# A hybrid attention block on eight cores: split exponentials without own waits, norm rows sent through memory, and a new order of chunks and squares

## The reference, cut to what matters

```python
xn = rmsnorm(x, norm_mix_g[l])
u = xn @ w_in[l]                      # b_g, c_g, v_a | q, k, v | gates
y_a = short_gated_conv(b_g, c_g, v_a, conv_w[l]) @ w_a_out[l]
o = diff_attention(q, k, v, lam, slopes)      # 4 heads, two softmax maps each, ALiBi, causal
o = rmsnorm(o, subln_g[l]) * (1.0 - lam_init)
y_b = o.reshape(Bsz, S, DIFF_WIDTH) @ w_b_out[l]
x = x + (g_a * y_a + g_b * y_b) @ w_o[l]
h = rmsnorm(x, norm_mlp_g[l]) @ w_mlp_in[l]
x = x + jnp.square(jax.nn.relu(h)) @ w_mlp_out[l]
return rmsnorm(x, norm_final_g)
```

## Time and profile before

| what | us |
|---|---|
| median of 3 runs (lowest, highest) | 1164.12 (1163.68, 1166.56) |
| the profiled execution's own time | 1163.79 |
| its span on core 5, the slowest (spans of the eight cores 1160.2 to 1162.2) | 1162.2 |
| PE busy in the span | 1127.2 |
| DVE, ACT, POOL busy | 466.9, 550.3, 84.3 |

### The profile page before, as it was taken

The page is one execution under the profiler, slowest core; times in us unless marked ns, Lnnn a source line. Parts: engine busy times, 40 slices in busy tenths (PEclk is TensorE's granted clock), DMA queues, the critical chain, the costliest instruction groups (busy, mean ns, idle before and its releaser), DMA issues.

```text
span 1162.2 us, 20430 instructions; the slowest of 8 cores (1160.2 to 1162.2 us)
## 1 busy us (share of the span) xinstructions
PE 1127.2 (97%) x7162; PEld 563.0 (48%) x7162; DVE 466.9 (40%) x1051; ACT 550.3 (47%) x760; POOL 84.3 (7%) x136
## 2 busy tenths in 40 slices
PE   7999999999999999999999999999999999999997
PEld 3444555455455555555544444444444444444444
DVE  2476666644654632433435544222221322223212
ACT  2585786676666888878523223321231033003301
POOL 5212001001001001001100001000000000000000
PEclk8999999999999999999999999999999999999999
DMA  9877522332067059375296686911210140012001
GB/s 140 166 144 138 144 90 51 110 56 46 5 132 147 19 99 179 65 191 105 38 253 168 207 165 172 158 43 55 70 57 1 55 111 17 19 55 73 2 37 55
DMA packets 67491, 111.46 MB, mean 96 GB/s; under 512 B 37216, under 2 KB 40288, under 8 KB 66368
## 3 DMA queue, kind: packets, MB, share of 16 engines
q0 software_dynamic: 15056, 40.22, 22.5%
q1 hardware_dynamic: 52192, 69.68, 20.0%
q10 hardware_dynamic: 144, 0.26, 0.1%
HBM read 114.40 MB, written 29.36 MB: 124 GB/s over the span
## 4 chain that ended last, share of the span: by engine, by line
PE 92%; ACT 3%; DVE 2%; issue 2%; DMA 1%; POOL 0%; DVEq 0%; ACTq 0%; POOLq 0%
PE ps_all L441 92%; ACT big L715 2%; DMA big<-wv 1%; DVE big L780 0%; DVE big L594 0%; DVE big L604 0%; POOL big L484 0%; ACT big L852 0%; DVE big L772 0%; DVE big L863 0%; DVE big L574 0%; ACT big L592 0%; POOL big L446 0%; DVEq L152 0%; DVE big L571 0%
## 5 line engine op out<-in xcount | busy, mean ns | idle before, releaser
L441 PE MATMUL ps_all<-big 128*128 128x512 bf16 (+7 forms) x7162 | 1127.2, 323 | 28.9 <-ACT big L715 8.2
L441 PEld LDWEIGHTS ps_all<-big 128*128 128x128 bf16 (+2 forms) x7162 | 563.0, 98 | 592.9 <-issue 100.7
L715 ACT ACTIVATE big<-ps_all,big 128x1024 bf16<-128x1024 f32 (+3 forms) x384 | 338.3, 926 | 111.4 <-PE ps_all L441 104.4
L982 ACT ACTIVATE big<-ps_all 128x512 bf16<-128x512 f32 x128 | 76.5, 598 | 137.6 <-PE ps_all L441 137.4
L983 DVE TENSOR_TENSOR big<-big 128x512 bf16<-128x512 bf16 x128 | 54.5, 426 | 156.5 <-ACT big L982 156.0
L999 ACT ACTIVATE big<-big 128x1024 bf16<-128x1024 f32 x15 | 15.9, 1057 | 187.9 <-DVE big L994 187.9
L863 DVE SCALAR_TENSOR_TENSOR big<-big,ps_all 128x512 f32<-128x512 f32 x64 | 43.7, 687 | 106.3 <-PE ps_all L441 106.3
L994 DVE SCALAR_TENSOR_TENSOR big<-ps_all,big 128x512 f32<-128x512 f32 x30 | 22.5, 752 | 143.5 <-PE ps_all L441 143.5
L852 ACT ACTIVATE big<-ps_all,big 128x512 f32<-128x512 f32 x64 | 43.6, 686 | 67.7 <-PE ps_all L441 66.6
L898 ACT ACTIVATE big<-big 128x1024 bf16<-128x1024 f32 x16 | 16.9, 1057 | 47.0 <-DVE big L893 47.0
L724 DVE TENSOR_TENSOR big<-big 128x256 bf16<-128x256 bf16 x64 | 18.5, 289 | 46.7 <-ACT big L715 46.6
(11 more groups left out here) (90 smaller groups left out, 296.8 us busy)
## 6 DMA issues: line engine op xcount, KB each, us to landing
big<-xs SPq DMA_DIRECT2D x36, 512.0 KB, 6.8
big<-w POOLq DMA_DIRECT2D x32, 512.0 KB, 8.1
xm_sp<-big SPq DMA_DIRECT2D x16, 512.0 KB, 3.8
big<-xm_sp SPq DMA_DIRECT2D x16, 512.0 KB, 5.8
big<-xT POOLq DMA_DIRECT2D x31, 256.0 KB, 7.6
out<-big SPq DMA_DIRECT2D x15, 512.0 KB, 2.7
xn_sp<-big SPq DMA_DIRECT2D x4, 1024.0 KB, 6.6
big<-wg POOLq DMA_DIRECT2D x8, 512.0 KB, 5.9
```

Source lines behind the costliest of these rows:

```text
L441: S.op("pe", lambda e: e.matmul(out, lhsT, rhs, start=start, stop=stop, skip_group_check=skip), reads, writes)
L715: act(lambda e, a=a, b=b, c=c, s=s, PT=PT, scale=scale: e.activation(PT.ap[:, :, a:b], Sb[s][:, :, a:b], AF.Exp, bias=ccol(C_BTAB + c), sc ...
L982: act(lambda e: e.activation(r.ap, ps, AF.Relu), key, [r])
```

## The change

1. `ex` marks its calls as parts, so the second call of a side no longer waits for the first; likewise the three copies to `o_raw`.
2. `bcast` of blocks 1, 2 and 3 goes. `row` stores the norms (128 partitions x 4) to `rs_sp` in DRAM and loads the row back onto 128 partitions, both from SP. It is the last step of `stats`, and `ksc` of the partner's blocks becomes a step of its own there.
3. In the first pair of a head `pv(n,0)` comes ahead of the chunk.
4. The squares of block 1 are spread over 7 chunks in place of 4; those of block 2 have at least a step of a weight load between them.
5. The copy of the halo goes from ACT to DVE.
6. `until` takes the banks so that the burst's last chunk has bank 7.

```diff
+    rs_sp = dscr("rs_sp", [4, 512], F32)
...
-            if blk in ksc:
-                dve(lambda e: e.tensor_scalar_mul(ksc[blk].ap, rs1[blk].ap, 0.125), [rs1[blk]], [ksc[blk]])
+
+        def scaled():
+            dve(lambda e: e.tensor_scalar_mul(ksc[blk].ap, rs1[blk].ap, 0.125), [rs1[blk]], [ksc[blk]])
...
-        return [sq(0), sq(1), sq(2), sq(3), last]
+        return [sq(0), sq(1), sq(2), sq(3), last, scaled if blk in ksc else lambda: row(blk)]
...
+    def row(blk):
+        settle("norm%d" % (blk % 2))
+        S.dma("sp", lambda e: e.dma_start(out=rs_sp[blk].rearrange("(t p) -> p t", p=128), in_=rs1[blk].ap, allow_slow_non_contiguous=True),
+              [rs1[blk]], ["rssp%d" % blk])
+        ld(R_b[blk % 2].ap, rs_sp[blk:blk + 1].partition_broadcast(128), [R_b[blk % 2]], ["rssp%d" % blk])
...
-            act(lambda e: e.copy(hh.ap[:, lo:hi, :], v[:, :, 0, :]), ck, [hh])
+            dve(lambda e: e.tensor_copy(hh.ap[:, lo:hi, :], v[:, :, 0, :]), ck, [hh])
...
+            S.parts.discard(PT)
             for a, b, c in parts:
                 act(lambda e, a=a, b=b, c=c, s=s, PT=PT, scale=scale: e.activation(
                     PT.ap[:, :, a:b], Sb[s][:, :, a:b], AF.Exp, bias=ccol(C_BTAB + c), scale=scale),
-                    Sk[s] + [cst] + ([ksc[blk]] if blk in ksc else []), [PT])
+                    Sk[s] + [cst] + ([ksc[blk]] if blk in ksc else []), [PT], True)
...
-    W += [(0, f) for f in normed(0)] + spread(ks(5)[1:], [])
-    W += spread(vs(5), [halo_stat] + stats(1, 2) + wc_load(0))
+    W += [(0, f) for f in normed(0)]
+    W += spread(ks(5)[1:] + vs(5), stats(1, 2) + [halo_stat] + wc_load(0))
     W += spread(vs(1), xT_steps(2, 2))
-    W += [(1, bcast(1))]
-    W += spread(ks(1) + qs(1), stats(2, None) + wc_load(1) + [halo_norm]
-                + wc_load(2) + wc_load(3) + [lambda t=t: tok_load(6, t) for t in range(4)])
+    s2 = stats(2, None)
+    W += spread(ks(1) + qs(1), [s2[0]] + wc_load(1) + [s2[1]] + wc_load(2) + [s2[2]] + wc_load(3)
+                + s2[3:] + [halo_norm] + [lambda t=t: tok_load(6, t) for t in range(4)])
...
-    def until(name, banks=range(8)):
+    def until(name, banks=range(8), turn=False):
         keep, oring[0] = oring[0], Ring(list(banks))
+        if turn:
+            oring[0].i = -sum(w for w, f in W[pos[0]:marks[name]]) % len(banks)
...
-                until(pairs[n + 1]["g"], (7, 0, 1, 2, 3))
+                until(pairs[n + 1]["g"], (0, 1, 2, 3, 7), True)
...
+        lead = p["first"] and n > 0
+        if lead:
+            pv(n, 0)
         if not p["last"]:
             work(2200 - (400 if diag else 0))
-        pv(n, 0)
+        if not lead:
+            pv(n, 0)
         pv(n, 1)
```

More of the change, by code:

```diff
@@ L103, in _add, with op @@
         return ev
-    def op(self, eng, fn, reads=(), writes=()):
-        return self._add(eng, fn, reads, writes, False)
+    def op(self, eng, fn, reads=(), writes=(), part=False):
+        return self._add(eng, fn, reads, writes, False, (), part)
     def dma(self, eng, fn, reads=(), writes=(), extra=(), part=False):
@@ L431, in flush_masks, with act, dve @@
             late_masks.pop(0)()
[L434 to L438, removed]
+    def act(fn, reads, writes, part=False):
+        S.op("act", fn, reads, writes, part)
+    def dve(fn, reads, writes, part=False):
+        S.op("dve", fn, reads, writes, part)
     def mm(out, lhsT, rhs, start, stop, reads, writes, skip=False):
@@ L752, in out @@
             dve(lambda e: e.tensor_copy(o[:, m, 0:3, 0:129], bank(4 + m)[:, 0:390].rearrange(
-                "p (t e) -> p t e", t=3)[:, :, 0:129]), [pk(4 + m)], [o_raw])
+                "p (t e) -> p t e", t=3)[:, :, 0:129]), [pk(4 + m)], [o_raw], True)
+        S.parts.discard(o_raw)
         out(0)
         dve(lambda e: e.tensor_copy(o[:, :, 3, 0:129], bank(6)[:, 0:260].rearrange(
-            "p (m e) -> p m e", m=2)[:, :, 0:129]), [pk(6)], [o_raw])
+            "p (m e) -> p m e", m=2)[:, :, 0:129]), [pk(6)], [o_raw], True)
         out(1)
@@ L1187, in build_program @@
     mark(0)
-    W += [(0, f) for f in normed(0)] + spread(ks(5)[1:], [])
-    W += spread(vs(5), [halo_stat] + stats(1, 2) + wc_load(0))
+    W += [(0, f) for f in normed(0)]
+    W += spread(ks(5)[1:] + vs(5), stats(1, 2) + [halo_stat] + wc_load(0))
     W += spread(vs(1), xT_steps(2, 2))
-    W += [(1, bcast(1))]
-    W += spread(ks(1) + qs(1), stats(2, None) + wc_load(1) + [halo_norm]
-                + wc_load(2) + wc_load(3) + [lambda t=t: tok_load(6, t) for t in range(4)])
+    s2 = stats(2, None)
+    W += spread(ks(1) + qs(1), [s2[0]] + wc_load(1) + [s2[1]] + wc_load(2) + [s2[2]] + wc_load(3)
+                + s2[3:] + [halo_norm] + [lambda t=t: tok_load(6, t) for t in range(4)])
     mark(1)
     W += [(0, f) for f in normed(1)]
-    W += spread(vs(2), []) + [(1, bcast(2))] + spread(ks(2)[:2], [])
+    W += spread(vs(2) + ks(2)[:2], [])
     c0 = [(1, f) for f in conv(0)]
@@ L1203, in build_program @@
     W += spread(conv(1)[:11], xT_steps(3, 1))
-    W += [(1, bcast(3))] + [(1, f) for f in conv(1)[11:]]
+    W += [(1, f) for f in conv(1)[11:]]
     W += spread(ks(3) + vs(3) + qs(3), xT_steps(7, 0) + stats(7, None))
```

## The result

The changed kernel took 1177.3 us (median, 1176.07 to 1178.73), the kernel before on the same chip 1164.05: a ratio of 1.011, 95% interval 1.009 to 1.013. The forecast was 1151.5. The profiled execution took 1178.73, which is 1.4 us above its median and 14.9 above the profiled execution of the kernel before; its span on the slowest core is 1177.2.

What follows compares the result with a forecast made beforehand. PE was taken as the bound, busy 1127.2 of 1162.2 us. Terms of 16.3 us less 3.3 and 0.7 coming back left 12.3, taking the profiled 1163.8 to 1151.5; range 1144 to 1160.

Steps and rivals of the forecast that it cites:

- The rows through memory: Each of three rows takes a store and a load on SP, about 14 us (6 to 38), costing nothing at 14.
- The third rival: Row 2 late for block 2's first key chunk: free to 19 us, 1161 at 29, slower from 32; chance 0.14.
- the worst case, 1170.5: Row 2's store and load both at their upper ends, 38 us together: PE loses 19 us, giving 1170.5.
- Products and short slots: Three bcast products go, 3.0 us; PE's waits for exponentials or mask after their short slots go, 2.4 us.
- Own waits: Exponentials without waits for their own engine shorten PE's waits for score banks, head 0 of groups 1 to 3: 2.9 us.
- the second rival: Removing own waits gives nothing, as the engine drains between calls anyway: the 2.9 falls away, 1154.4 us; chance 0.03.
- Scale, halo, squares: PE waits saved: ksc behind POOL's power 2.6 us, around the halo chunks 0.6, beside the squares of block 1 1.2.
- Value products ahead of the chunk: At twelve head starts eight value products cover PE's wait for bank 7: 3.0 us, between 0 and 3.2.
- Banks: In the burst into group 2 the last chunk no longer sits in a bank the scores need: 0.6 us.
- What comes back: A quarter of the 13.3 us of waits returns, 3.3, plus 0.7 in the burst into group 1.
- the first rival: PE's waits only move: two thirds of the 13.3 us come back, giving 1157.1 us; chance 0.20.

Runs made afterwards that it cites:

- experiment 5: Changed kernel with the row kept in partition order, stored as 128 pieces of 16 B and read in 16 B steps: 1155.67 us.
- experiment 6: Changed kernel with each row turned by an identity product and stored as 4 pieces of 512 B: 1153.64 us; with row 2 asked for earlier, 1154.92 us.
- the kernel with the products: Changed kernel with the three bcast products of blocks 1, 2 and 3 back and no row through memory: 1152.4 us.
- experiment 3: Kernel before with twelve extra stores of various piece sizes in the last stage, each followed by a one-element load: 1164.98 us.
- experiment 4: Kernel before with eleven extra last-stage stores, 4 B pieces at steps of 4 to 64 B and one of 512 B pieces: 1164.26 us.
- experiment 1: Changed kernel with bcast of blocks 1, 2 and 3 back in place of the rows through memory: 1152.4 us, ratio 0.9895.
- experiment 7: Changed kernel with no row for blocks 1 to 3, the readers taking the norms of block 0: 1147.5 us, ratio 0.985.

## Why the prediction was wrong

The step that failed is "The rows through memory", where it says of the rows "So it costs nothing by the value that I take". They cost 29.8 us. Three things in that step were wrong.

*The price of the store.* I took on_sp's landing, median 3.4, since both have 512 pieces. Its pieces are of 256 B. Pieces of 4 B side by side took 15 to 19 us in the change and 13 to 16 alone. At row 2 the median was too low whatever the pieces, since behind the spill larger ones too took 10 us (experiments 5 and 6). I had read the warning, and filed it behind the sum: the Trainium skill (DMA: Bandwidth & Descriptors, Rules for kernel authors) advises against a strided last dimension, as each element becomes a descriptor. The trace agrees with the rule, with 2016 more packets on SP's hardware queue in the changed kernel than the 52192 of the kernel with the products; but experiments 3 and 4 show that the count alone is not the harm, since 512 pieces 64 B apart took 2.9 to 7.7 us.

*The path of row 2.* Store and load took 30.6 us, inside my bounds of 6 to 38. The third rival priced this: free up to 19 us, so 11.6 of PE's time, and PE lost 13.07 at the place it named (at 143.8 us for DVE, where I had said about 125). Its condition, that "both upper ends must meet", was wrong as a reason for a chance of 0.14: at 15.45 and 15.16 neither was at its upper end of 19.9 and 18.3, and both were slow in one stretch, perhaps because the first holds up the second.

*Rows 1 and 3.* "Rows 1 and 3 are ready many slots ahead" is true, and no engine waited for them. They cost all the same, 3.95 and 5.33 us of PE and the slow clock behind, while the store held up every transfer of the core. Without the rows these waits are gone (experiments 1 and 7); by which way the stand reached PE stays open. No rival had this, nor a term for the clock (7.0 us in all), and so the range's upper end and even the worst case, 1170.5, were too low.

The rest of the forecast, by its steps, was right in sum and in part in its terms. With the row free the kernel took 1147.5, a gain of 17.2 on the before of that comparison (1164.7), where the terms gave 16.3; that the sum fits is in part luck, since the two terms that are off cancel. *Products and short slots*: 5.4 forecast, 4.9 measured. *Own waits*: 2.9, and 5.2 measured, with the copies in it; the second rival (nothing) is out. The Trainium skill's rule for that rival (VectorE: DVE Perf Modes, The DRAIN you can't avoid) says that leaving out the semaphore between VectorE's calls gains nothing. This case's trace does not agree: DVE's three copies took 1.36 us without own waits and 1.82 with them. How much of the 5.2 is theirs and how much ACT's was not tried. *Scale, halo, squares*: 4.4, and 4.5 measured. *Value products ahead of the chunk*: 3.0, and 0.9 measured, as much as PE's idle time fell; the waits at the chunk went, and others grew. *Banks*: 0.6, and 1.0. These measured terms make 16.5, and the 0.7 that is left of 17.2 is less than they are uncertain by. *What comes back*: I let 4.0 return, and apart from the lead's waits nothing did, so the first rival is out as well.

## What to carry to other kernels

Before a value of a few kilobytes goes through memory, look at the pieces in which it is stored: 4-byte pieces side by side held the transfers of the core for 8 to 17 us, the same values as 4 rows of 512 B took 1.2 to 2.4 us where nothing else was in the way. A transfer that nobody waits for is free only while it holds up nobody else's; in the last stage the stores of experiment 3 cost nothing; in the attention rows 1 and 3, for which nobody waited, cost PE some 14 us, by their waits and the slow clock behind. And a price that is taken from another row needs the same size of piece, not only the same number.

## What was not expected of the hardware

- Packets of 4 B were through the DMA engines at some 9 ns each, and yet the core's queues landed next to nothing for 8 to 17 us.
- The time hangs on the distance of the pieces: at one place 13.0, 6.7, 3.9 and 3.6 us at steps of 4, 8, 32 and 64 B.
- Engines with no wait in the program stood still up to 5.5 us within such a stand, in the attention; in the last stage PE did not.
- Leaving out DVE's own waits between three copies took them from 1.82 us to 1.36.
- All eight cores stored at nearly the same time. Whether one core alone would stand as long was not tried.
